# Moving a state space block between the k steps of two projections, with PSUM banks given by hand

## The chip, the cores and the metric

The kernel runs on one core of one Trainium2 chip. The metric is the device time of one execution in microseconds. Before the change the median of three runs is 1287.9 us (1287.57 to 1289.54).

## The reference

A model of two layers on 512 tokens of width 1024. Each layer adds to the stream a mixer, a cross attention to 256 memory rows, and a mixture of experts. The change is in the mixer of the first layer:

```
z = rmsnorm(h) @ w_in                       # 512 x 1024 @ 1024 x 1536
uv = gelu(z[:, :1024])
ya = gmlp(uv[:, :512], uv[:, 512:])         # u * (causal chunk mixing of layernorm(v) + bias)
yb = s5(z[:, 1024:])                        # diagonal complex state space model, 32 groups of 16
h += concat(ya, yb) @ w_out
...
lam_bar = exp(lam * step); bu = uf @ b_bar  # complex states, 64 per group
states = scan(a * state + bu)
y = gelu(real(states @ c) + d * uf)
yb = y * sigmoid(y @ w_glu + b_glu)
```

Everything is fp32. The kernel runs the state space model in chunks of 8 tokens, 64 chunks: inside a chunk a fixed 128 x 128 matrix for each group (s5T) maps inputs to outputs, and only the state at chunk borders is scanned.

## The kernel before

Each engine has its own program, written out by hand, and signals and waits by semaphores. PSUM has eight banks of 128 x 512 fp32. A list, `uses_of_banks`, names every use of a bank in the order of TensorE's program, with a count; without a group the uses go round all eight banks in turn, with a group (a tuple) they take its banks. `claim` lets TensorE wait until the earlier use of the bank was evacuated, `fill` signals the result, `await_filled` waits for it on the reading engine, `evac` gives the bank back, and `taken` waits for that.

Projections of the width 1024 run in `split_gemm`: eight k steps, and in each, for each of the four token tiles, three fp32r passes (high times high, high times low, low times high), so 12 matmuls of 128 x 512 to a step, which accumulate in four banks. The high parts of the weights are made by ScalarE (L1353, `weights`) and the low parts by GpSimd (L659, `low_parts`), into a ring of four steps; a high part waits until the step four earlier was used. `split_gemm` takes `between`, a table from a k step to functions that are called after it; the second layer's mixer uses it already.

The first mixer has three projections: ev2 (the state space input s5u), ev1 (v0) and ev0 (u0). TensorE's order before is: ev2, the transposes into chunks, V (L922, chunk inputs into states, 64 small products), Vsw (L929, the product with `perm`, which exchanges real and imaginary halves, four products of two recorded parts each), the whole of ev1, Xp (L936, the same exchange of the scanned states), y (L945 and L946, chunk outputs: for each of 8 banks four groups, the inputs by s5T and the carried states by s5PP), the whole of ev0, yT (L955), then mixed (L963, the token mixing of the LayerNorm of v).

VectorE multiplies the Vsw banks by sines (L1926), runs the scan and products (L1929 to L1936, `s5_scan`), subtracts the Xp banks (L1942) and signals `s5_x`; then it works on the LayerNorm of v (L1949 to L1959, `vh_ready`), for which ScalarE makes 16 squares (L1482) and a root (L1485). ScalarE copies V (L1409) after `s5_t`, the sixteen-part signal of the eight transfers L605 that build s5T out of memory which V's copy overwrites; it applies Gelu to v0 (L1469), to the eight y banks (L1474), and to u0 (L1490).

In the second layer `mix_norm1` transposes the normalised stream into eight banks (L777), ScalarE and VectorE split each into high (L1345) and low (L1770), and `dq` is the first projection of that mixer, in banks 4 to 7.

Of the kernel before, what the change touches and what calls it, by code (L numbers as in the profile page):

```python
# [27 lines left out]
ACT = mybir.ActivationFunctionType  # L28
# [10 lines left out]
def uses_of_banks(layers):  # L39

    steps = [("cols", 1), ("memT", 4), ("kv0", 2), ("ct", 2), ("kv1", 2), ("kv2", 2), ("bT", 8), ("mix_norm0", 8),
# [3 lines left out]

    def attention(l):
        return [(f"xa_norm{l}", 8), (f"q{l}", 8), (f"qT{l}", 8), (f"sc{l}", 8), (f"pT{l}", 8), (f"o{l}", 8),
                (f"wo{l}", 8)]

    def moe(l):  # L50
        return [(f"ffn_norm{l}", 8), (f"route{l}", 1), (f"logits{l}", 1), (f"rank{l}", 1), (f"idx{l}", 1, (7,)), (f"gslot{l}", 1, (7,))]

    G, O = (1, 2, 3, 4), (5, 6, 7, 0)
    steps += attention(0) + moe(0)
    steps += [("mix_norm1", 8), ("dq", 4, (4, 5, 6, 7)), ("if", 1, (0,)), ("dk", 4, G), ("qk", 4, O), ("col", 1, (1,)),
              ("qk1", 4, G), ("og", 4, O), ("v", 4, G), ("mlh0", 4, O), ("mlh1", 4, O), ("dT", 8, O),
              ("dv", 4, G), ("ms0", 4, O), ("num0", 4, O), ("mlh2", 4, O), ("mlh3", 4, O), ("ms1", 4, O), ("num1", 4, O),
              ("ms2", 4, O), ("mt0", 3, O), ("mt1", 3, O), ("mo0", 1, G), ("ms3", 4, O), ("mo1", 1, G), ("mt2", 3, O),
              ("ycT", 4, O), ("out1", 4, G), ("mo2", 1, O), ("mt3", 3, O), ("mo3", 1, O), ("out1b", 4, O)]
    steps += attention(1) + moe(1)  # L60
    first, bank_of, nth_of = {}, [], []
    used, turn = [0] * 8, {None: 0, G: 0, O: 0}
    for name, k, *group in steps:
        first[name] = len(bank_of)
        for i in range(k):
            g = group[0] if group else None
            if g in turn:
                b = g[turn[g] % 4] if g else turn[g] % 8
                turn[g] += 1
            else:  # L70
                b = g[i]
            bank_of.append(b)
            nth_of.append(used[b])
            used[b] += 1
    return first, bank_of, nth_of


def program(nc, A, out):
# [8 lines left out]
    LC = P // GI  # L87
    NC = T // LC
# [5 lines left out]
    first, bank_of, nth_of = uses_of_banks(2)  # L94
    RING = 4

    ctx = ExitStack()
    with ctx:
# [80 lines left out]
        S = {n: sem(n) for n in names}  # L179
# [8 lines left out]
        def bank(u):  # L188
            return banks[bank_of[u]]
# [15 lines left out]
        def await_filled(eng, u):  # L205
            eng.wait_ge(filled[bank_of[u]], nth_of[u] + 1)

        def evac(ins, u):
            ins.then_inc(evacuated[bank_of[u]], 1)
# [134 lines left out]
        Y = E[2][0:NC, :].rearrange("c (j n) -> c j n", j=LC)  # L344
        s5Wst = v3(hflat, G)
        uT = v3(E[4], 4, 0, 2048)
        yT = v3(E[3], 4, 2048, 4096)
# [111 lines left out]
        xlo = {"ev": v3(E3r, KT), "q": v3(E4r, KT), "o": v3(E1r, KT), "od": v3(E2r, KT), "out1": v3(E5r, KT, 0, KT * T)}  # L459
        xhi, ohi = v3(xTr, KT), v3(E0r, KT)  # L460

        def by_k(buf):
            return [buf[:, k, :] for k in range(KT)]
# [299 lines left out]
        def _(pe):  # L763
# [16 lines left out]
            def split_gemm(u, panel_name, hi, lo, x_ready=None, weights_first=False, between={}):  # L780


                for k in range(KT):
                    s_ = step(panel_name, k)
                    if x_ready:
                        x_ready(k)
                    pe.wait_ge(S["w_lo"], s_ + 1)
                    wh, wl = whi[s_ % RING], wlo[s_ % RING]
                    xh, xl = hi[k], lo[k]
                    for t in range(TT):  # L790
                        if k == 0:
                            claim(pe, u + t)
                        c = slice(t * P, (t + 1) * P)
                        if weights_first:
                            passes = ((wh[:, c], xh), (wh[:, c], xl), (wl[:, c], xh))
                        else:
                            passes = ((xh[:, c], wh[:, :]), (xh[:, c], wl[:, :]), (xl[:, c], wh[:, :]))
                        for n, (a, b) in enumerate(passes):
                            ins = pe.matmul(bank(u + t)[:, :], a, b, start=(k == 0 and n == 0),  # L799
                                            stop=(k == KT - 1 and n == 2))  # L800
                        if k == KT - 1:
                            fill(ins, u + t)
                    if k < KT - 1:
                        ins.then_inc(S["w_used"], 1)
                    for step_between, n in between.get(k, ()):
                        step_between(n)
# [3 lines left out]
            u = first["cols"]  # L810
# [7 lines left out]
            u = first["memT"]  # L818
# [23 lines left out]
            for n, c in enumerate((Cst1, Cst2)):  # L842
                u = first["ct"] + n
# [8 lines left out]
            for n in range(8):  # L852
                u = first["bT"] + n
# [12 lines left out]
            for n in range(8):  # L866
                u = first["w"] + n
# [49 lines left out]
            for n in range(4):  # L917
# [4 lines left out]
                    ins = pe.matmul(bank(u)[:, g * NC:(g + 1) * NC], s5Q[:, 8 * n + g, :], Uc[:, 8 * n + g, :],  # L922
                                    start=(g == 0), stop=(g == 7), skip_group_check=True)
                fill(ins, u)
            for n in range(4):
                u = first["Vsw"] + n
                claim(pe, u)
                taken(pe, first["V"] + n)
                fill(pe.matmul(bank(u)[:, :], perm[:], Vc[:, 8 * n:8 * n + 8, :].rearrange("p g c -> p (g c)"),  # L929
                               start=True, stop=True), u)  # L930
            split_gemm(first["v0"], "ev1", by_k(xhi), by_k(xlo["ev"]))
            pe.wait_ge(S["s5_scan"], 1)
            for n in range(4):
                u = first["Xp"] + n
                claim(pe, u)
                fill(pe.matmul(bank(u)[:, :], perm[:], Vs[:, 8 * n:8 * n + 8, :].rearrange("p g c -> p (g c)"),  # L936
                               start=True, stop=True), u)
            pe.wait_ge(S["s5_x"], 1)
            pe.wait_ge(S["s5_t"], 16 * LC)
            for n in range(8):  # L940
                u = first["y"] + n
                claim(pe, u)
                for g in range(4 * n, 4 * n + 4):
                    o = bank(u)[0:NC, (g % 4) * P:(g % 4 + 1) * P]
                    pe.matmul(o, Uc[:, g, :], s5T[:, g, :], start=(g % 4 == 0), stop=False, skip_group_check=True)  # L945
                    ins = pe.matmul(o, Sc[:, g, :], s5PP[:, g, 1:LC + 1, :].rearrange("p k i -> p (k i)"),  # L946
                                    start=False, stop=(g % 4 == 3), skip_group_check=True)
                fill(ins, u)
            split_gemm(first["u0"], "ev0", by_k(xhi), by_k(xlo["ev"]))
            taken_all(pe, "y", 8)  # L950
            for n in range(4):
                u = first["yT"] + n
# [377 lines left out]
        def _(act):  # L1330
# [16 lines left out]
            def weights(name, k0, k1):  # L1347

                await_panel(act, name)
                for k in range(k0, k1):  # L1350
                    s_ = step(name, k)
                    await_ring(act, s_)
                    act.activation(whi[s_ % RING][:, :], slot(name)[:, k, :], ACT.Copy).then_inc(S["w_hi"], 1)  # L1353
# [112 lines left out]
            for n in range(4):  # L1466
                u = first["v0"] + n
                await_filled(act, u)
                evac(act.activation(Gv[:, n, :], bank(u)[:, :], ACT.Gelu_apprx_tanh), u)  # L1469
            act.wait_ge(S["s5_x"], 1)  # L1470
            for n in range(8):
                u = first["y"] + n
                await_filled(act, u)
                evac(act.activation(Y[:, :, 64 * n:64 * n + 64].rearrange("c j (g i) -> c g j i", g=4),  # L1474
                                    bank(u)[0:NC, :].rearrange("c (g j i) -> c g j i", g=4, j=LC),
                                    ACT.Gelu_apprx_tanh), u)
            for n in range(16):
                if n % 4 == 0:
                    weights("ev0", RING + n // 4, RING + n // 4 + 1)
                if n == 0:  # L1480
                    act.wait_ge(S["ln_mean"], 1)
                a_(act.activation(junk[:, 0:P], Gv[:, n // 4, (n % 4) * P:(n % 4 + 1) * P], ACT.Square,  # L1482
                                  bias=xnm[:, n:n + 1], accum_out=xsum[:, n:n + 1]), "ln_sq")
# [968 lines left out]
```

## Time and profile before

| | us |
|---|---|
| median of three runs | 1287.9 |
| profiled execution, its own time | 1289.58 |
| its span, first to last instruction | 1287.4 |
| TensorE busy (matmul) | 1191.6 |
| VectorE busy | 612.5 |
| ScalarE busy | 500.0 |
| GpSimd busy | 346.8 |
| mean granted TensorE clock | 0.974 of full |

All times below are of the one profiled execution, in microseconds from its first instruction. An entry of the chain of waits gives start, length and what the time was spent in; TensorE's matmuls overlap, so a length in the chain is the time to the next one, while the length in a timeline includes the pipeline's end.

### The profile page before, as it was taken

The numbers are of one execution on the slowest core, as the hardware profiler recorded it, in microseconds if no ns is written. First come the engines' busy times: TensorE is split into PE (matmuls) and PEld (weight loads), VectorE is DVE, ScalarE is ACT, GpSimd is POOL, SyncE is SP. The second block draws the span as 40 slices with busy tenths as digits, with TensorE's granted clock in tenths as the row PEclk, the third lists the DMA queues.
The fourth block names the chain that finished last, engine by engine and source line by source line (L and its number), as shares of the span: only waits on it lengthen the run. The fifth ranks groups of instructions, "written<-read, shape, count | busy, mean of one in ns | idle before, by whom it ended". The sixth has DMA issues, their size and how long they took to land.

```text
span 1287.4 us, 14453 instructions
## 1 busy us (share of the span) xinstructions
PE 1191.6 (93%) x5099; PEld 847.9 (66%) x5099; DVE 612.5 (48%) x1117; ACT 500.0 (39%) x980; POOL 346.8 (27%) x311
## 2 busy tenths in 40 slices
PE   5999899999899799999699999979998997999997
PEld 2467686788667555555477887758887674555554
DVE  5883433320512644445735972772205226444457
ACT  2453146354624323233434354352546343233222
POOL 2023331564022011112134754253350220111120
PEclk9999899999899899999989999999999998999999
DMA  9432221276102899999103221012311017999953
GB/s 267 143 131 74 30 107 66 107 300 247 66 1 96 326 395 369 377 382 339 67 13 126 79 89 42 1 66 69 128 66 66 1 67 314 409 380 379 378 218 142
DMA packets 77639, 222.70 MB, mean 173 GB/s; under 512 B 21708, under 2 KB 22648, under 8 KB 65272
## 3 DMA queue, kind: packets, MB, share of 16 engines
q1 hardware_dynamic: 64688, 180.22, 38.0%
q0 software_dynamic: 10048, 36.74, 7.5%
q10 hardware_dynamic: 2840, 4.91, 1.0%
q8 instruction: 39, 0.64, 0.2%
q14 instruction: 24, 0.20, 0.0%
HBM read 187.90 MB, written 32.51 MB: 171 GB/s over the span
## 4 chain that ended last, share of the span: by engine, by line
PE 77%; DVE 12%; ACT 5%; issue 2%; POOL 1%; SPq 1%; DMA 1%; DVEq 0%; POOLq 0%; ACTq 0%
PE bank L799 37%; PE bank L1114 16%; PE bank L1141 7%; PE bank L1028 2%; PE bank L1069 1%; PE bank L835 1%; DVE h L2202 1%; PE bank L1042 1%; PE bank L972 1%; DVE E2r L2163 1%; PE bank L777 1%; PE bank L1019 1%; PE bank L1164 1%; SPq L605 1%; ACT E2r L1589 1%
## 5 line engine op out<-in xcount | busy, mean ns | idle before, releaser
L659 POOL TENSOR_TENSOR wlo<-W,whi 128x512 fp32r<-128x512 f32 x176 | 255.0, 1461 | 492.2 <-ACT whi L1353 491.8
L1353 ACT ACTIVATE whi<-W 128x512 fp32r<-128x512 f32 x176 | 107.9, 633 | 256.1 <-PE bank L799 249.1
L799 PE MATMUL bank<-whi,xTr 128*128 128x512 f32 x480 | 191.2, 398 | 0.6 <-ACT E L1716 0.6
L799 PE MATMUL bank<-wlo,xTr 128*128 128x512 f32 x416 | 162.7, 391 | 0.0
L1114 PE MATMUL bank<-W,E 128*128 128x512 f32 x256 | 114.4, 601 | 1.9 <-DVE E L2036 1.9
L1114 PE MATMUL bank<-E 128*128 128x512 f32 x256 | 112.4, 592 | 0.0
L799 PEld LDWEIGHTS bank<-whi,xTr 128*128 128x128 f32 x480 | 90.7, 189 | 20.5 <-issue 1.3
L1141 PE MATMUL bank<-whi,E2r 128*128 128x512 f32 x256 | 87.4, 402 | 8.9 <-DVE E2r L2163 8.4
L799 PEld LDWEIGHTS bank<-wlo,xTr 128*128 128x128 f32 x416 | 78.6, 189 | 16.7 <-issue 1.0
L692 POOL COPY idx<-slots 128x1 uint32 (+1 forms) x30 | 5.5, 182 | 307.8 <-PE bank L1103 217.6
L1114 PEld LDWEIGHTS bank<-W,E 128*128 128x128 f32 x256 | 49.0, 193 | 57.9 <-issue 54.4
L1114 PEld LDWEIGHTS bank<-E 128*128 128x128 f32 x256 | 48.7, 190 | 54.7 <-issue 53.5
L1811 DVE TENSOR_TENSOR h<-bank,h 128x512 f32<-128x512 f32 x32 | 21.8, 692 | 131.4 <-PE bank L799 131.4
L1141 PEld LDWEIGHTS bank<-whi,E2r 128*128 128x128 f32 x256 | 48.1, 188 | 25.5 <-issue 10.5
L1589 ACT ACTIVATE E2r<-bank 128x256 fp32r<-128x256 f32 x32 | 12.3, 384 | 132.4 <-PE bank L1124 132.4
L799 PE MATMUL bank<-whi,E0r 128*128 128x512 f32 x160 | 63.1, 395 | 0.0
L799 PE MATMUL bank<-whi,E1r 128*128 128x512 f32 x160 | 62.8, 393 | 0.0
L2163 DVE TENSOR_TENSOR E2r<-bank,E2r 128x256 fp32r<-128x256 f32 x32 | 13.6, 424 | 102.9 <-ACT E2r L1589 102.9
L799 PE MATMUL bank<-whi,E2r 128*128 128x512 f32 x160 | 62.5, 391 | 0.0
L835 PE MATMUL bank<-W,E 128*128 128x512 f32 x128 | 58.8, 621 | 4.0 <-DVE E3r L1770 2.5
L799 PE MATMUL bank<-wlo,E0r 128*128 128x512 f32 x160 | 62.4, 390 | 0.0
L1602 ACT ACTIVATE E<-bank 128x512 f32<-128x512 f32 x26 | 15.5, 597 | 97.1 <-PE bank L1141 97.1
(465 smaller groups left out, 2256.9 us busy)
## 6 DMA issues: line engine op xcount, KB each, us to landing
E<-in_moe_w SPq DMA_DIRECT2D x48, 1024.0 KB, 9.4
W<-in_moe_w SPq DMA_DIRECT2D x32, 1024.0 KB, 9.2
xT<-in_moe_w SPq DMA_DIRECT2D x16, 1024.0 KB, 10.9
W<-in_od_w_in SPq DMA_DIRECT2D x7, 2048.0 KB, 8.4
ybuf<-E SPq DMA_DIRECT2D x26, 512.0 KB, 5.1
ybuf<-memV POOLq DMA_DIRECT2D x12, 1024.0 KB, 19.9
W<-in_w_mem_kv SPq DMA_DIRECT2D x4, 2048.0 KB, 8.1
W<-in_xa_wq SPq DMA_DIRECT2D x4, 2048.0 KB, 7.6
```

Of the source, the lines that this page charges most:

```text
L605: sp.dma_start(s5T[GI * j:GI * (j + 1), :, GI * j:P], s5Wst[0:GI, :, 0:P - GI * j])\
L659: pool.tensor_tensor(wlo[s_ % RING][:, :], slot(name)[:, k, :], whi[s_ % RING][:, :].bitcast(F32), ALU.subtract).then_inc(S["w_lo"], 1)
L799: ins = pe.matmul(bank(u + t)[:, :], a, b, start=(k == 0 and n == 0), stop=(k == KT - 1 and n == 2))
L835: ins = pe.matmul(bank(u)[:, :], memnT[:, k, t * P:(t + 1) * P], slot(f"kv{n}")[:, k, :], start=(k == 0), stop=(k == KT - 1))
L1028: ins = pe.matmul(bank(u)[:, :], memV[:, k, n * XD + d * P:n * XD + (d + 1) * P], pT[:, n, k, :], start=(k == 0), stop=(k == 1))
L1114: ins = pe.matmul(banks[2 + par][:, :], xgT[par][:, k, :], w13s[j][:, :, k, :], start=(k == 0), stop=(k == KT - 1))
L1141: ins = pe.matmul(banks[5 + half][:, :], a, b[:, :], start=(k == 0 and n == 0), stop=(k == 1 and n == 2))
L1353: act.activation(whi[s_ % RING][:, :], slot(name)[:, k, :], ACT.Copy).then_inc(S["w_hi"], 1)
L1589: act.activation(hThi[par], banks[4][:, 0:2 * P], ACT.Copy).then_inc(m["ht_hi"], 1)
L1602: act.activation(yo[par][:, 512:1024], banks[6][:, :], ACT.Copy).then_inc(m["y_ready1"], 1)
L1811: evac(tt(hs, bank(u)[:, :], hs, ALU.add), u)
L2163: tt(hTlo[j % 2], banks[4][:, 0:2 * P], hThi[j % 2].bitcast(F32), ALU.subtract).then_inc(m["ht_ready"], 1)
```

## The change

The exchanges Vsw come after k step 1 of the projection ev1. Xp comes after k step 0 of ev0, and the eight y banks in pairs after its k steps 1 to 4. The banks of V, Vsw, v0, Xp, y and u0 are given by hand. On ScalarE the high parts of ev0's steps 4 and 5 are made ahead of the first y Gelu, each pair of y Gelus stands ahead of a group of four squares, and the high parts of steps 6 and 7 come after the second and third pair.

```
-             ("uc1", 1), ("uj3", 2), ("uc2", 1), ("uc3", 1), ("V", 4), ("Vsw", 4), ("v0", 4), ("Xp", 4), ("y", 8),
-             ("u0", 4), ("yT", 4), ("mixed", 4), ("glu0", 2), ("yaT", 4), ("glu2", 2), ("out0", 8)]
+             ("uc1", 1), ("uj3", 2), ("uc2", 1), ("uc3", 1), ("V", 4, (0, 1, 2, 3)), ("Vsw", 4, (0, 1, 2, 3)), ("v0", 4, (4, 5, 6, 7)),
+             ("Xp", 4, (4, 5, 6, 7)), ("y", 8, (4, 5, 6, 7, 4, 5, 6, 7)), ("u0", 4, (0, 1, 2, 3)), ("yT", 4), ("mixed", 4), ("glu0", 2), ("yaT", 4), ("glu2", 2), ("out0", 8)]
...
-            for n in range(4):
+            def swapped(n):
                 u = first["Vsw"] + n
...
-            split_gemm(first["v0"], "ev1", by_k(xhi), by_k(xlo["ev"]))
-            pe.wait_ge(S["s5_scan"], 1)
-            for n in range(4):
+
+            def swapped_back(n):
...
-            pe.wait_ge(S["s5_x"], 1)
-            pe.wait_ge(S["s5_t"], 16 * LC)
-            for n in range(8):
+
+            def chunk_outputs(n):
+                pe.wait_ge(S["s5_x"], 1)
+                pe.wait_ge(S["s5_t"], 16 * LC)
...
-            split_gemm(first["u0"], "ev0", by_k(xhi), by_k(xlo["ev"]))
+
+            split_gemm(first["v0"], "ev1", by_k(xhi), by_k(xlo["ev"]), between={1: [(swapped, n) for n in range(4)]})
+            split_gemm(first["u0"], "ev0", by_k(xhi), by_k(xlo["ev"]),
+                       between={0: [(swapped_back, n) for n in range(4)], 1: [(chunk_outputs, 0), (chunk_outputs, 1)],
+                                2: [(chunk_outputs, 2), (chunk_outputs, 3)], 3: [(chunk_outputs, 4), (chunk_outputs, 5)],
+                                4: [(chunk_outputs, 6), (chunk_outputs, 7)]})
             taken_all(pe, "y", 8)
...
+            weights("ev0", RING, RING + 2)
             act.wait_ge(S["s5_x"], 1)
-            for n in range(8):
-                u = first["y"] + n
-                await_filled(act, u)
-                evac(act.activation(Y[:, :, 64 * n:64 * n + 64].rearrange("c j (g i) -> c g j i", g=4),
-                                    bank(u)[0:NC, :].rearrange("c (g j i) -> c g j i", g=4, j=LC),
-                                    ACT.Gelu_apprx_tanh), u)
             for n in range(16):
                 if n % 4 == 0:
-                    weights("ev0", RING + n // 4, RING + n // 4 + 1)
+                    for y in (n // 2, n // 2 + 1):
+                        u = first["y"] + y
+                        await_filled(act, u)
+                        evac(act.activation(Y[:, :, 64 * y:64 * y + 64].rearrange("c j (g i) -> c g j i", g=4),
+                                            bank(u)[0:NC, :].rearrange("c (g j i) -> c g j i", g=4, j=LC),
+                                            ACT.Gelu_apprx_tanh), u)
+                if n in (4, 8):
+                    weights("ev0", RING + 1 + n // 4, RING + 2 + n // 4)
```

## Rows read from the trace of the kernel before

**Rows 1.** The page, chain that ended last, shares by engine.

```profile
PE 77%; DVE 12%; ACT 5%; issue 2%; POOL 1%; SPq 1%; DMA 1%; DVEq 0%; POOLq 0%; ACTq 0%
```

**Rows 2.** Busy time by stage: window, length, each engine's busy us (count), clock, DMA.

```profile
core 0: us, PE busy (x) PEld busy (x) DVE busy (x) ACT busy (x) POOL busy (x), PEclk, DMA share, GB/s
129.00:136.50 7.50, 7.21 (x64) 7.07 (x64) 0.00 (x0) 0.56 (x1) 0.00 (x0) 1.00 0.73 95
136.50:140.40 3.90, 0.00 (x0) 0.00 (x0) 0.00 (x0) 0.66 (x2) 0.00 (x0) 0.88 0.39 54
140.40:147.00 6.60, 6.52 (x9) 2.83 (x10) 2.08 (x3) 1.41 (x3) 0.00 (x0) 0.55 0.00 0
149.00:169.00 20.00, 20.00 (x89) 16.49 (x88) 17.56 (x8) 4.56 (x8) 18.26 (x6) 1.00 0.01 1
```

**Rows 3.** Chain that ended last, from V to y: start, length, what.

```profile
136.47 3.25 DMA E<-h
...
140.48 6.57 PE bank L929 x8
147.05 21.79 PE bank L799 x96
168.84 3.45 PE bank L936 x8
...
173.23 0.43 PE bank L945 x2
```

**Rows 4.** Timeline of TensorE, the V products (in brackets idle time and releaser).

```profile
128.85 7.36 PE L922 MATMUL bank<-E 128*128 128x64 f32 x64
```

**Rows 5.** The same chain from u0 on.

```profile
187.42 21.98 PE bank L799 x96
209.40 2.16 PE bank L955 x32
211.56 3.63 PE bank L963 x8
```

**Rows 6.** Timeline of GpSimd, the last low part before V.

```profile
111.85 1.26 POOL L659 TENSOR_TENSOR wlo<-W,whi 128x512 fp32r<-128x512 f32 x1 [1.43 <-ACT whi L1353]
```

**Rows 7.** Timeline of ScalarE, 139 to 202 us.

```profile
139.74 2.06 ACT L1409 ACTIVATE h<-bank 128x512 f32<-128x512 f32 x4 [10.18 <-DMA E<-h]
...
169.52 1.28 ACT L1469 ACT_TABLE_LOAD   x1
170.81 2.07 ACT L1469 ACTIVATE E<-bank 128x512 f32<-128x512 f32 x4
...
187.46 0.59 ACT L1474 ACTIVATE E<-bank 64x512 f32<-64x512 f32 x1 [1.16 <-PE bank L946]
...
191.00 0.39 ACT L1482 ACTIVATE junk<-E,st 128x128 f32<-128x128 f32 x1
...
192.87 0.19 ACT L1482 ACTIVATION_READ_ACCUMULATOR junk<-E,st 128x1 f32 x1
...
201.06 0.18 ACT L1482 ACTIVATION_READ_ACCUMULATOR junk<-E,st 128x1 f32 x1
```

**Rows 8.** Timeline of VectorE: behind the scan, and the last LayerNorm step.

```profile
163.47 3.27 DVE L1936 TENSOR_TENSOR h<-E 128x2048 f32<-128x2048 f32 x1
...
207.73 2.29 DVE L1959 TENSOR_TENSOR E<-E,W 128x2048 f32<-128x2048 f32 x1
```

**Rows 9.** Second mixer: chain pieces between k steps, and two stages with the clock.

```profile
806.35 2.77 PE bank L799 x12
809.12 4.46 PE bank L1265 x40
813.59 2.73 PE bank L799 x12
...
801.00:824.00 23.00, 22.79 (x110) 16.95 (x111) 13.77 (x46) 8.55 (x23) 7.65 (x6) 1.00 0.01 1
824.00:846.00 22.00, 21.33 (x115) 16.80 (x114) 17.88 (x66) 8.96 (x27) 1.26 (x1) 1.00 0.00 1
```

**Rows 10.** mix_norm1 to dq: VectorE's low parts of k=4 to 7, and the chain.

```profile
652.24 2.73 DVE L1770 SCALAR_TENSOR_TENSOR E2r<-bank,cols,xTr 128x512 fp32r<-128x512 f32 x4
...
652.86 21.78 PE bank L799 x96
```

More of the change, by code:

```diff
@@ L930, in _ @@
                                start=True, stop=True), u)
-            split_gemm(first["v0"], "ev1", by_k(xhi), by_k(xlo["ev"]))
-            pe.wait_ge(S["s5_scan"], 1)
-            for n in range(4):
+            def swapped_back(n):
+                pe.wait_ge(S["s5_scan"], 1)
                 u = first["Xp"] + n
```

## The prediction

> **What bounds the kernel now.** I read the page first. The chain that ended last runs through TensorE for 77% of the span and VectorE for 12% [rows 1]: time goes away only where TensorE stands still or runs slowly. So I cut the stretch that the change touches, from the state-input products (L922) to the token mixing (L963), into stages, and looked in each for idle time and clock.
>
> There are three losses in it. After the last V product TensorE idles and then the clock is low: the stage from 136.5 has no matmul at all, and the one from 140.4 ran at a granted clock of 0.55, mostly the lower of its two levels, though the stages before and after are at 1.00 [rows 2]. The chain says what it waited for: the L605 transfers landed at 139.72, ScalarE could then copy V into the space they had been reading, and the eight swap products L929 began at 140.48 and took 6.57 us, where the same eight products with the same operand shapes took 3.45 us later (L936) [rows 3]. V itself ended at 128.85 + 7.36 = 136.21 [rows 4]. The third is the wait behind L936: it ended at 172.29 and L945 began at 173.23 [rows 3]. From there to L963 TensorE has no gap: y, u0 and the transposes stand end to end [rows 3, 5].
>
> The times from 136.21 to 211.56, where L963 starts, are: 4.27 idle, 6.57 swap, 21.79 v0, 3.45 swap back, 0.94 idle, 14.19 y (173.23 to 187.42), 21.98 u0, 2.16 yT; together 75.35, as it must be [rows 3, 5].
>
> **The change part by part.** *Swaps between k steps 1 and 2 of v0.* Steps 0 and 1 of ev1 wait for nothing late: their banks 4 to 7 were last used by uc0, uj2 and uc1, which had to be evacuated for V to be computed, and the ring's first four low parts were made by 113.1, before V [rows 6]. One k step is 12 matmuls, 21.79/8 = 2.72 us [rows 3], so two fill 136.21 to 141.66. ScalarE copies V from 139.74 to 141.80 [rows 7], one bank each 0.52 us, so the first swap (141.66) finds bank 0 done and each next one too. The 4.27 us idle goes. TensorE never stands still, so I take the swap at the full-clock 3.45 us: 3.12 less. V moves from banks 4 to 7 to 0 to 3, free since uj3, uc2, uc3: nothing. Behind the waiting swap only v0's steps 2 to 7 are queued; the ring feeds them: ScalarE starts on step 4 at 141.8, and it is needed at 145.11 + 5.45 = 150.6.
> v0 ends at 136.21 + 3.45 + 21.79 = 161.45.
>
> *Swap back behind step 0 of u0.* Its vector chain starts when the swaps are evacuated, at about 146.2 instead of 147.9, and so s5_scan, which came with L1936's start at 163.47 [rows 8], comes near 161.8. u0's step 0 ends at 164.17, so the wait is covered. New is that the swap back uses v0's banks and must wait for the Gelu of v0: before, v0 ended at 168.84 and the first Gelu began, behind a high part and a table load of 1.28 us, at 170.81, 0.52 each [rows 3, 7]. So bank 4 is free 2.5 us after v0's end, at 163.95, 0.2 us before it is wanted, and the others follow faster than the 0.86 us of a product. Cost 0. Without step 0 as cover this would be 2.5 us; if the claim waited for all four Gelus it would be 161.45 + 4.04 - 164.17 = 1.3 us, the upper bound.
>
> *y in pairs behind steps 1 to 4.* The 0.94 us wait goes: the swap back ends at 167.62, VectorE finishes it 0.7 us later, and y starts only after step 1, at 170.35. y has four banks instead of eight; a bank is wanted again a whole k step after its pair, while its Gelu is finished 0.6 us after its fill (187.42 to 188.05 for the last) [rows 7]. Nothing again. The high parts of steps 4 to 7 now stand between the y Gelus in ScalarE's queue, as do four squares after each pair; the latest, step 7, is made after y5's Gelu (about 187.5), and TensorE wants it near 199. Covered by 10 us.
>
> *Returns to the projection.* Each piece between ends with a change of operand kind. After the swap v0 took 21.79 us, eight plain steps; after y u0 took 21.98, so that return cost 0.19 [rows 3, 5]. In the second mixer, built this way already, the step after 40 L1265 products took 2.73, that after L1275 2.77 or less: 0.01 to 0.05 [rows 9]. I take 0.19 for the four returns after y, the same pair of instructions, of which one existed: 0.57 added, with 0.05 for three more (0.15) and 0.19 for five more (0.95) as the bounds. The Trainium skill (TensorE: Matmul & The Clock Gate, "Step-by-step: what each phase is for") says that weight loads are pulled ahead of running matmuls; by that a return would be free and the sum 0.57 us better. The 21.98 here says otherwise after y.
>
> u0 ends at 161.45 + 21.79 + 3.45 + 14.19 + 4 x 0.19 = 201.64 instead of 209.40; yT ends at 203.80.
>
> *What is late next: the LayerNorm.* It used to be hidden under u0. vh_ready needs all 16 squares, and the last four now stand behind the Gelus of y6 and y7. y7 is filled three steps and a return before u0's end: 201.64 - 8.17 - 0.19 = 193.28. Gelu 0.64, four squares 2.06 (191.00 to 193.06) [rows 7]. From the last square to vh come the root, the reciprocal, 16 scalings and the gain: the squares ended at 201.24 and L1959 at 207.73 + 2.29 = 210.02, so 8.8 us [rows 7, 8]. So 193.28 + 0.64 + 2.06 + 8.8 = 204.8, against 203.80: L963 waits 1.0 us. Bounds: 0, and 1.7, a third of the 2.06 us of squares more. L963 starts at 204.8 instead of 211.56: **6.8 us earlier**. Behind it the order is as before.
>
> *The banks elsewhere.* The six uses given by hand took 28 turns, so each later use in plain rotation moves by four banks. In the first layer every use moves alike and meets its old predecessor. Where the rotation meets groups fixed by hand it doesn't: mix_norm1 had k 0 to 7 in banks 3,4,5,6,7,0,1,2 and now has 7,0,1,2,3,4,5,6, and dq stands in 4 to 7. dq's first tile needed the evacuation of k=1, and will need that of k=5, its second k=6, its third k=7. VectorE did k=4 to 7 from 652.24 to 654.97, so k=5 is done at about 653.65, k=6 at 654.3; dq began at 652.86 [rows 10]. So **0.85 us later**; the tiles follow at 0.68 each and find 654.3 and 654.97 met. Bounds 0.8 and 2.1 (all evacuated first). xa_norm1 also moves against out1b, but its transposes come after the evacuations either way: 0.
>
> The SP queue only gets its signals sooner (glu panel with v0's end, x again with s5_x), and the panels are wanted later than they land: 0.
>
> **Sum.** -4.27 - 3.12 - 0.94 + 0.57 + 1.0 + 0.85 = -5.9 us. The profiled execution's span 1287.4 becomes 1281.5 and its own time 1289.58 becomes 1283.7. The median of the runs is 1287.9, 1.7 under that execution, and my time is **1282.0**.
>
> **Rivals.** *A, new waits eat half.* The margin of 0.2 us before the swap back is thin, and dq may wait for all evacuations: +1.3, +1.25, +0.7 in the LayerNorm, 3.25 if all comes, so up to 1285.3. Against it: the Gelu and evacuation rows are steady. *B, v0's first steps don't start early,* because a bank, a panel or a low part is late: then the idle time and the low clock stay and the costs come all the same: -0.94 + 0.57 + 1.0 + 0.85 = +1.5, so 1289.4. Nothing in the profile speaks for it. *C, slower: the clock falls in the interleaved stretch.* Place: from u0's step 0 to step 4. Work at the lower of the two levels (1.2 instead of 2.4 GHz) takes twice the time, as the swaps show (6.57 against 3.45). If only the 14.19 us of y ran so, the time would be 1282.0 + 14.2 = 1296.2; from 8.5 us of such work on the kernel is slower beyond what can be told. For it: a TensorE that moves between banks, with a wait at each piece. Against it: the second mixer does the same with six kinds of pieces, and its stretches from 801 to 846 were at 1.00 in spite of a wait [rows 9]. The Trainium skill (TensorE: Matmul & The Clock Gate, "A second HAM failure mode: psum-queue depth-cycling") speaks against the change: it tells of a kernel that cycled through PSUM banks and whose small idles made the clock swing. By that rule it would be C; the stretches of [rows 9] weigh more.
>
> **How the numbers follow.** The forecast has 0.74, A 0.14, B 0.05, C 0.04, and 0.03 is for more gain than forecast. The forecast's own range is 1280.8 to 1283.5 (returns and LayerNorm at their bounds, and half a us for where clock changes fall elsewhere). The three runs spread by 2 us; a difference under 0.2%, 2.6 us, can't be told from none. A reaches to 1285, and the range is 1280.4 to 1285.0. Faster by over 0.2% is all of the forecast and most of A, 0.90; the same 0.06; slower 0.04.
>
> **What would show it.** Right: TensorE busy without a gap from 128.9 to about 204, L929 near 3.5 us at clock 1.00, v0 ending near 161.5, u0 near 201.6, a wait of about 1 us for L1959 at L963, one of about 0.8 us before dq, and everything else moved rigidly. Wrong: a wait at L936 for the Gelu of v0 or at y for L1942, a clock under 1 between 141 and 204, u0's steps well over 2.72 us, or a later stage that gives the time back.

## The result, and the profile after

Five runs of the changed kernel had a median of 1281.13 us (1280.2 to 1283.53), five of the kernel before 1288.69; the ratio is 0.9943, with a 95% interval from 0.9931 to 0.9956. Two later comparisons of the same two kernels gave 0.9949 (0.9935 to 0.9962) and 0.9948 (0.9934 to 0.9962). By the three ratios the change takes off 6.6 to 7.4 us; 5.9 were forecast. The profiled execution took 1280.32 us with a span of 1278.1, 9.3 less than the span before, and this pair of traces is taken apart below, since 9.3 is more than the runs bear out.

The chain that ended last in the changed kernel, from V on (start, length, what; L922 V, L929 and L936 the two exchanges, L946 and L947 y, L961 yT, L969 the token mixing):

```profile
127.33 7.29 PE bank L922 x64
134.62 5.55 PE bank L799 x24
140.17 3.43 PE bank L929 x8
143.60 19.05 PE bank L799 x84
...
162.66 3.67 PE bank L936 x8
166.33 2.75 PE bank L799 x12
169.09 0.36 PE bank L946 x2
...
172.72 2.94 PE bank L799 x12
...
192.46 8.38 PE bank L799 x36
200.85 2.16 PE bank L961 x32
203.01 0.94 issue
203.95 3.67 PE bank L969 x8
```

The idle time of [rows 3] is gone, and the first exchange takes 3.43 us instead of 6.57. TensorE stands still only once, 0.94 us ahead of L969. From V's end to L969 it is 203.95 - 134.62 = 69.33 us instead of 75.35, 6.02 less. The busy time by stage (window, length, busy us by engine with counts, clock, DMA) shows full clock all the way, where [rows 2] had 0.55:

```profile
127.40:134.60 7.20, 7.20 (x65) 7.20 (x66) 0.00 (x0) 0.57 (x1) 0.00 (x0) 1.00 0.73 95
...
140.10:143.60 3.50, 3.50 (x10) 1.58 (x9) 2.08 (x3) 1.20 (x3) 2.50 (x2) 1.00 0.01 2
...
162.60:192.40 29.80, 29.79 (x186) 24.10 (x185) 5.95 (x8) 13.36 (x38) 8.15 (x6) 1.00 0.29 106
```

What the wait of 0.94 us is for stands in the timelines of ScalarE and VectorE: the last y Gelu, and the last step of the LayerNorm (L1967 here, L1959 in [rows 8]), which ends at 203.85, 0.1 us before L969 starts:

```profile
192.50 0.59 ACT L1483 ACTIVATE E<-bank 64x512 f32<-64x512 f32 x1 [1.09 <-PE bank L947]
...
201.56 2.29 DVE L1967 TENSOR_TENSOR E<-E,W 128x2048 f32<-128x2048 f32 x1
```

Ahead of dq the chain now goes over VectorE:

```profile
633.33 5.16 DVE E L1792 x4
...
638.53 3.05 PE bank L777 x13
...
642.32 2.10 DVE E2r L1778 x3
...
644.56 1.61 PE bank L799 x6
```

From the start of the scaling (L1792, before L1784) to dq it is 11.23 us. In the trace of before the chain goes from the scaling over the transposes straight to dq at 652.86 [rows 10], and 652.86 - 642.39 = 10.47, so dq comes 0.76 us later than it did:

```profile
642.39 5.16 DVE E L1784 x4
647.59 5.27 PE bank L777 x29
```

The whole difference of the two profiled spans, cut at V's end, L969, the scaling and dq, is then -1.6 (136.21 to 134.62) - 6.0 - 1.5 + 0.8 - 1.0 = -9.3 us. In that order the pieces are: up to V's end, V to L969, L969 to the scaling, the scaling to dq, and behind dq. The touched pieces make -5.3; the other -4.0 (1.59 + 1.45 + 1.00) lie in stages whose instructions did not change.

### The profile page after: what moved, and what is told of

Its sections match the earlier page's. It is cut to its first block, busy times and chain, and to the rows that moved or that the text cites. A ratio compares the mean times of both kernels' runs of the same rounds, so it can differ in the third digit from the quotient of the medians.

```text
span 1278.1 us, 14465 instructions
## 1 busy us (share of the span) xinstructions
PE 1185.6 (93%) x5099; PEld 843.2 (66%) x5099; DVE 612.1 (48%) x1117; ACT 500.6 (39%) x980; POOL 347.5 (27%) x311
## 4 chain that ended last, share of the span: by engine, by line
PE 78%; DVE 12%; ACT 5%; issue 3%; POOL 1%; DMA 1%; DVEq 0%; POOLq 0%; ACTq 0%
PE bank L799 37%; PE bank L1120 16%; PE bank L1147 7%; PE bank L1034 2%; PE bank L1075 2%; PE bank L1048 1%; PE bank L835 1%; DVE h L2210 1%; PE bank L978 1%; DVE E2r L2171 1%; PE bank L1170 1%; ACT E2r L1597 1%; PE bank L1025 1%; PE bank L1281 1%; PE bank L777 1%
## 5 line engine op out<-in xcount | busy, mean ns | idle before, releaser
L1120 PE MATMUL bank<-W,E 128*128 128x512 f32 x256 | 112.9, 594 | 1.9 <-DVE E L2044 1.9
L835 PE MATMUL bank<-W,E 128*128 128x512 f32 x128 | 57.4, 609 | 3.7 <-DVE E3r L1778 2.2
```

The costliest lines, as they stand in the source:

```text
L835: ins = pe.matmul(bank(u)[:, :], memnT[:, k, t * P:(t + 1) * P], slot(f"kv{n}")[:, k, :], start=(k == 0), stop=(k == KT - 1))
L1120: ins = pe.matmul(banks[2 + par][:, :], xgT[par][:, k, :], w13s[j][:, :, k, :], start=(k == 0), stop=(k == KT - 1))
```

## The experiments

All ratios are to runs of the kernel before on the same chip. Where a figure says V to mixing, it is the time from the end of V (L922) to the start of the token mixing, 75.35 us before and 69.33 changed.

**The first exchange alone.** The exchange moves behind k step 1 of v0; the swap back, y and u0 keep their old order.

```
-             ("uc1", 1), ("uj3", 2), ("uc2", 1), ("uc3", 1), ("V", 4), ("Vsw", 4), ("v0", 4), ("Xp", 4), ("y", 8),
-             ("u0", 4), ("yT", 4), ("mixed", 4), ("glu0", 2), ("yaT", 4), ("glu2", 2), ("out0", 8)]
+             ("uc1", 1), ("uj3", 2), ("uc2", 1), ("uc3", 1), ("V", 4, (0, 1, 2, 3)), ("Vsw", 4, (0, 1, 2, 3)), ("v0", 4, (4, 5, 6, 7)),
+             ("Xp", 4, (0, 1, 2, 3)), ("y", 8, (4, 5, 6, 7, 0, 1, 2, 3)), ("u0", 4, (4, 5, 6, 7)), ("yT", 4, (0, 1, 2, 3)), ("mixed", 4), ("glu0", 2), ("yaT", 4), ("glu2", 2), ("out0", 8)]
...
-            split_gemm(first["v0"], "ev1", by_k(xhi), by_k(xlo["ev"]))
+            split_gemm(first["v0"], "ev1", by_k(xhi), by_k(xlo["ev"]), between={1: [(swapped, n) for n in range(4)]})
```

> Only the first exchange (L929 of before) moves between k steps 1 and 2 of v0; swap back, y and u0 keep their old order, and banks are given so that every later use has its old bank. Theory: the 4.3 us idle and the 3.1 us of low clock go, so v0 ends 7.4 us earlier, but the scan on VectorE comes only 1.7 us earlier, so the swap back and y wait for it for about 2.4 us: 5.0 us less than before, no change before dq. Rival 1: the whole gain of the change is in this move, 7.4 us less. Rival 2: the gain is due to the second half of the change, no gain here.

Measured: ratio 0.9955 (0.9942 to 0.9969), median 1282.59. Chain:

```profile
136.10 5.54 PE bank L799 x24
141.65 3.45 PE bank L929 x8
...
161.52 3.25 DVE h L1937
...
164.98 2.46 DVE E L1943 x4
...
167.67 0.43 PE bank L946 x2
...
183.53 22.01 PE bank L799 x96
...
207.70 3.63 PE bank L964 x8
```

Busy time by stage, the first part of y:

```profile
167.60:172.30 4.70, 4.63 (x28) 4.63 (x29) 2.46 (x2) 0.59 (x1) 0.00 (x0) 0.65 0.79 257
```

The exchange is as cheap as forecast, and now the chain runs over VectorE's scan. The wait ahead of y, 2.7 us, was foreseen; not foreseen was that it brings the clock down, so that y took 183.53 - 167.67 = 15.86 us instead of 14.19. V to mixing is 71.60, 3.75 less than before instead of the 5.0 expected. Rival 1 falls in the trace: this half needs the other one to hide the scan. The times alone would not exclude rival 1: the interval reaches from 4.0 to 7.5 us. The measured 5.8 us lies above the trace's 3.75; the traced execution is the slowest of its five (1284.90), so the others need not have had the drop at y. The second half of the change is worth 71.60 - 69.33 = 2.3 us by the traces, and 1.4 when its 0.9 ahead of dq is taken off; the times of this version and of the changed kernel overlap and don't show it.

**The u0 part alone.** The first exchange is called four times in front of v0, as before; all else is the changed kernel.

```
-            split_gemm(first["v0"], "ev1", by_k(xhi), by_k(xlo["ev"]), between={1: [(swapped, n) for n in range(4)]})
+            for n in range(4):
+                swapped(n)
+            split_gemm(first["v0"], "ev1", by_k(xhi), by_k(xlo["ev"]))
```

> The first exchange goes back in front of v0; swap back and y pairs stay between the steps of u0, banks as in the changed kernel. Theory: the idle time and low clock are back, and what this half saves (0.94 us in front of y) is less than it costs (entries and returns around each piece, about 1.0 to 1.5, LayerNorm wait 0.9, dq 0.8): 1.5 to 2.5 us slower than before. Rival 1: this half is worth 2 us or more by itself, faster than before. Rival 2: neither, within 0.5 us.

Measured: ratio 1.0009 (1.0000 to 1.0018), median 1289.42. Chain:

```profile
140.60 6.28 PE bank L929 x8
146.88 24.52 PE bank L799 x108
...
211.78 0.93 issue
212.71 3.67 PE bank L971 x8
```

From the first exchange's start to the mixing it is 72.11 us, before 211.56 - 140.48 = 71.08: 1.0 more, and the banks ahead of dq come on top, 11.32 us from the scaling to dq instead of 10.47. That is 1.9 us in the trace, as expected. The time rose by about 1.2 us (0 to 2.3), at the edge of what can be told. So this half alone gains nothing; in the changed kernel its use is to stand over the scan.

**The idle time filled.** The order of before, with five more products in the gap:

```
+            claim(pe, first["Vsw"])
+            for _ in range(5):
+                pe.matmul(bank(first["Vsw"])[:, :], perm[:], s5Q[:, 0:4, :].rearrange("p g c -> p (g c)"),
+                          start=True, stop=True)
```

> The kernel before with five more products of the exchange's shape (128 x 512 fp32) in the idle time between V and the first exchange, into the bank that the exchange overwrites; order and banks unchanged. They add work and change no result. Theory: the idle time ends no earlier, but the clock stays up and the exchange takes 3.45 instead of 6.57 us: 3.1 us less than before. Rival 1: the exchange is slow for another reason (its operand just copied, the waits in between), then it stays at 6.57 us and the time is the same or up to 0.3 us longer. Rival 2: the five products run into the exchange's start and eat the gain.

Measured: ratio 0.9977 (0.9968 to 0.9986), median 1285.08. Chain (L927 the added products, L933 the exchange):

```profile
134.53 4.35 PE bank L927 x10
138.88 3.65 PE bank L933 x8
...
207.06 3.63 PE bank L967 x8
```

Busy time by stage, the exchange:

```profile
138.90:142.50 3.60, 3.60 (x9) 1.69 (x10) 2.08 (x3) 1.27 (x3) 0.00 (x0) 1.00 0.00 0
```

With more work the kernel is faster by 3.0 us. The exchange itself is 2.9 us shorter, at a clock of 1.00 instead of 0.55, and V to mixing is 72.53 us, 2.8 less. The exchange starts 4.35 us behind V's end instead of 4.27, so the added products delay it by only 0.1 us, and both rivals fall. That the first exchange was slow by the clock, and the clock low by the idle time, is shown. The Trainium skill (TensorE: Matmul & The Clock Gate, "HAM oscillation — how this bites in real kernels") says that idle gaps throttle the engine again; here the traces agree, with a clock of 0.55 behind the idle 4.27 us and 1.00 where they are filled.

**The banks alone**, in the order of before.

```
-             ("uc1", 1), ("uj3", 2), ("uc2", 1), ("uc3", 1), ("V", 4), ("Vsw", 4), ("v0", 4), ("Xp", 4), ("y", 8),
-             ("u0", 4), ("yT", 4), ("mixed", 4), ("glu0", 2), ("yaT", 4), ("glu2", 2), ("out0", 8)]
+             ("uc1", 1), ("uj3", 2), ("uc2", 1), ("uc3", 1), ("V", 4, (0, 1, 2, 3)), ("Vsw", 4, (0, 1, 2, 3)), ("v0", 4, (4, 5, 6, 7)),
+             ("Xp", 4, (4, 5, 6, 7)), ("y", 8, (4, 5, 6, 7, 4, 5, 6, 7)), ("u0", 4, (0, 1, 2, 3)), ("yT", 4), ("mixed", 4), ("glu0", 2), ("yaT", 4), ("glu2", 2), ("out0", 8)]
```

> The order of before with the changed kernel's bank list. Theory: the swap back must wait for the Gelus of v0 without a k step as cover, 2.5 us, and dq begins 0.8 us late: 3.3 us slower than before. Rival 1: the banks cost nothing, same time. Rival 2: y on four banks waits for its own Gelus as well, 5 us or more slower.

Measured: ratio 1.0033 (1.0021 to 1.0045), 4.2 us slower. Chain:

```profile
170.33 0.61 ACT E L1469
...
171.07 3.69 PE bank L936 x8
```

The swap back waits for v0's first Gelu, until 171.07, 2.7 us behind v0's end at 168.36. Step 0 of u0 as cover is what makes these banks free in the changed kernel, where L936 follows at once. y takes 14.19 us again (175.70 to 189.89), so rival 2 falls. V to mixing is 2.5 us more than before, and the scaling to dq 0.9 more: the trace has 3.4 of the 4.2 us.

**The changed kernel again, and the kernel before again.**

> The changed kernel once more, as the base for the three kernels run with it. Theory: 7 us less than before, of which 5.3 are made in the stages that the change touches and the rest by where the clock falls in stages that it does not touch; so this execution's trace should show 5.3 us again in the touched stages and another figure elsewhere. Rival: the other 2 us are a lasting effect of the moved banks, and come again in the same stages.

> The changed kernel a third time. Theory: 5 to 6 us less than before, 76.7 us from V's first product to L963, the drop near 70 us there or not. Rival: again 6.5 us or more, so that something outside the touched stages gains steadily.

> The kernel before once more as a candidate of its own. Theory: ratio 1.000 to the other runs of before within 0.15%; its trace shows the same low clock at 140 us, and the drops near 70 and 450 us may be there or not, 1.6 us each. Rival: these drops are in every execution of before, then they belong to this kernel and the changed one has rid itself of them.

Measured: the changed kernel 0.9949 and 0.9948, the kernel before 0.9998 (0.9989 to 1.0007). V to mixing is 69.32 and 69.30 us in the two new traces of the changed kernel, so in the changed kernel this stretch repeats to 0.1 us. In the second trace of before it is 74.94 instead of 75.35, because the exchange took 6.12 us instead of 6.57. Dq came 11.20 and 11.41 us behind the scaling in the new traces of the changed kernel, and 10.35 in that of before. Over all pairs the touched stages make 4.6 to 5.3 us. What does not repeat is shown by one window of the first trace of before, whose code no kernel here changes,

```profile
60.00:80.00 20.00, 17.53 (x85) 11.35 (x84) 19.54 (x29) 15.14 (x37) 4.97 (x4) 0.91 0.29 105
```

and the same window of the changed kernel:

```profile
60.00:80.00 20.00, 17.83 (x90) 11.71 (x89) 19.54 (x29) 15.16 (x37) 4.98 (x4) 1.00 0.29 105
```

V starts at 128.7 to 128.9 where the first kind is met and at 127.2 or 127.3 where the second is. Of 14 traces 8 have the one and 6 the other: both of before, and one of three of the changed kernel, have the drop. It is worth the 1.6 us of the first piece above. The -1.5 us between L969 and the scaling are the sum of three. In the first trace of before they are these rows of the chain (32 transposes of the attention, 64 small products, 16 products of an expert):

```profile
345.49 6.43 PE bank L1019 x32
...
430.06 8.81 PE bank L1069 x64
...
450.34 8.70 PE bank L1114 x16
```

In the first trace of the changed kernel the same instructions took 5.35, 9.96 and 7.13 us: -1.1, +1.2 and -1.6. The last is a drop of the clock at 440 to 460 us (0.91 against 1.00); four of the 14 traces have it, and in just these the 64 products ahead of it took 8.7 to 9.0 us instead of 9.9 to 10.3, so most of what it costs is given back. The transposes took 6.43 and 6.20 us in the traces of before and 5.35 in all three of the changed kernel, but 6.62 in the version with the lowest median below. Behind dq the changed kernel took 633.5, 636.1 and 633.7 us, before 634.5 and 634.4; the long one is in the execution of 1284.68 us, whose unchanged stages together gained nothing.

The theory of these experiments is confirmed for the touched stages. For the whole kernel the rival's number holds, again 6.6 us or more; that its cause is the moved banks is not shown, and the banks alone speak against it, since their time rose by more than their trace has. Three comparisons gave 6.6 to 7.4 us, and 4.6 to 5.3 are accounted for. The mean granted clock, which is on record for most executions, bears on the rest. The share of the full clock that was not granted, times the span, is on average 30.9 us in 51 executions of before and 26.2 us in the 15 of the changed kernel (mean clock 0.976 and 0.980). By [rows 2] the stages around the first exchange make 3.4 of these 4.7 us. So 1.3 us, an estimate with an error of 0.5, were gained by the clock in other stages. But the version with the idle time filled, with 25.9 us, shows the same gain and is not faster than its trace explains, so this does not show the cause of the rest either.

**y in one block.**

```
-                       between={0: [(swapped_back, n) for n in range(4)], 1: [(chunk_outputs, 0), (chunk_outputs, 1)],
-                                2: [(chunk_outputs, 2), (chunk_outputs, 3)], 3: [(chunk_outputs, 4), (chunk_outputs, 5)],
-                                4: [(chunk_outputs, 6), (chunk_outputs, 7)]})
+                       between={0: [(swapped_back, n) for n in range(4)], 1: [(chunk_outputs, n) for n in range(8)]})
...
-                if n % 4 == 0:
-                    for y in (n // 2, n // 2 + 1):
+                if n == 0:
+                    for y in range(8):
```

> The changed kernel with all eight y banks behind k step 1 of u0 and all eight Gelus ahead of the squares. Theory: three entries and three returns less, 1.0 us, and the LayerNorm is ready before u0 ends, so its wait of 0.9 us goes: 1.9 us less than the changed kernel. Rival 1: y on four banks in one block waits for its Gelus: up to 2 us more. Rival 2: the wait for the LayerNorm comes from something else and stays: 1.0 us less.

**mix_norm1's banks as before.**

```
-    steps += [("mix_norm1", 8), ("dq", 4, (4, 5, 6, 7)), ("if", 1, (0,)), ("dk", 4, G), ("qk", 4, O), ("col", 1, (1,)),
+    steps += [("mix_norm1", 8, (3, 4, 5, 6, 7, 0, 1, 2)), ("dq", 4, (4, 5, 6, 7)), ("if", 1, (0,)), ("dk", 4, G), ("qk", 4, O), ("col", 1, (1,)),
```

> The changed kernel with the banks of mix_norm1 given by hand as they were before the change. Theory: dq starts right behind the transposes again, 0.8 us less than the changed kernel. Rival: dq waits for something else too, no difference in the trace.

**Both.**

> Both edits, y in one block and mix_norm1's banks as before. Theory: the two add up, 2.7 us less than the changed kernel, 8.0 us less than before in the touched stages. Rival: they cover each other or the time is made up again later, 1 us less or nothing.

Measured beside the changed kernel's 1282.45 (0.9949): 1281.04 (0.9944, 0.9930 to 0.9958) for one block, 1282.73 (0.9949, 0.9936 to 0.9963) for the norm banks, 1280.99 (0.9942, 0.9929 to 0.9956) for both edits. The intervals overlap, so the times tell none of them from the changed kernel; the traces do. Chain of the one-block version:

```profile
136.28 5.53 PE bank L799 x24
...
170.73 0.36 PE bank L946 x2
...
184.85 16.54 PE bank L799 x72
...
203.55 0.67 issue
204.22 5.37 PE bank L967 x8
```

V to mixing is 67.94 us, 1.4 less than the changed kernel, of the 1.9 expected. y took 184.85 - 170.73 = 14.12 us, so its banks cost no wait and rival 1 falls. The entries and returns are saved, but the wait for the LayerNorm only fell from 0.94 to 0.67 us. With all squares behind the last Gelu it is 16 of them, not four, that stand between y and the root; that I had left out. Chain of the version with mix_norm1's banks alone, ahead of dq:

```profile
635.95 5.16 DVE E L1792 x4
...
641.15 5.13 PE bank L777 x29
646.29 3.90 PE bank L799 x17
```

The VectorE piece is gone from the chain, and the scaling to dq takes 10.34 us instead of 11.23: the banks cost 0.9 us there, as forecast. With both edits V to mixing is 67.96 us and the scaling to dq 10.43, so in the trace the savings add up to 2.2 us, of the 2.7 expected; the medians differ by 1.5, which the intervals don't tell from nothing.

**Squares between the Gelus.** Both edits, and on ScalarE two squares behind each y Gelu:

```
             for n in range(16):
+                if n % 2 == 0:
+                    u = first["y"] + n // 2
+                    await_filled(act, u)
+                    evac(act.activation(Y[:, :, 32 * n:32 * n + 64].rearrange("c j (g i) -> c g j i", g=4),
...
             a_.n["ln_sq"] += 1
+            weights("ev0", RING + 2, RING + 4)
```

> Y in one block and mix_norm1's banks as before, and now two of the LayerNorm's squares behind each y Gelu, the root right behind them, and the high parts of steps 6 and 7 after the root. Theory: in the version with both edits the LayerNorm still came 0.67 us late because 16 squares stood behind the last Gelu; now its root runs 8 us earlier, the wait in front of L963 goes and the stage from V to L963 is 0.7 us shorter than in that version, 74.6 us from V's first product instead of 75.3; some 9 us less than before in the touched stages. Rival 1: the wait has another cause and stays at 0.67 us. Rival 2: the high parts of steps 6 and 7 come late and TensorE waits inside u0.

Measured: ratio 0.9946 (0.9932 to 0.9960), median 1280.46, the lowest of all. Chain:

```profile
134.53 5.55 PE bank L799 x24
...
183.09 16.54 PE bank L799 x72
...
201.80 3.63 PE bank L967 x8
```

The wait is gone, so it was the LayerNorm's. V to mixing is 67.27 us, 2.1 less than the changed kernel, and u0's steps run without a gap. That it is faster as a whole the runs don't show: 1280.46 beside 1280.87 for the changed kernel in the same comparison, and beside 1280.99 for both edits without this one. Its trace has the drop at 440 us and the long transposes in the attention.

**One step of cover less.**

```
-            split_gemm(first["v0"], "ev1", by_k(xhi), by_k(xlo["ev"]), between={1: [(swapped, n) for n in range(4)]})
+            split_gemm(first["v0"], "ev1", by_k(xhi), by_k(xlo["ev"]), between={0: [(swapped, n) for n in range(4)]})
```

> The changed kernel with the first exchange behind k step 0 of v0 instead of step 1, so one step of cover less. Theory: ScalarE's copy of V sets the start, TensorE idles about 1.5 us, the clock stays up, and everything behind is 1.5 us later than in the changed kernel. Rival 1: the short idle time is enough to bring the clock down, then 3 us more on top. Rival 2: one step of cover is enough, no difference.

Measured: median 1285.16, ratio 0.9985 (0.9972 to 0.9998). Chain:

```profile
138.88 3.67 PE bank L929 x8
```

Busy time by stage, around the idle time:

```profile
137.00:139.00 2.00, 0.50 (x3) 0.16 (x2) 0.00 (x0) 0.87 (x2) 0.00 (x0) 1.00 0.16 21
```

TensorE idled 1.5 us in that window and the clock stayed at 1.00; the exchange took 3.67. From V's end to L936 it is 1.8 us more than in the changed kernel, which fits the theory that the copy of V sets the start, and the second step of cover is worth that. The traced execution, 1284.34, is 3.5 us slower than that of the changed kernel in the same comparison, and the trace has them: 1.8, and 1.7 in the mixing, which took 5.37 instead of 3.67 us at a clock of 0.68 behind the same 0.94 us wait. The medians differ by 4.3 us; the runs reached up to 1292.37, and the rest is open.

## Why the prediction was right

*The idle time and the clock, -4.27 and -3.12.* Right, and each shown by itself. With the gap filled the exchange is 2.9 us shorter, of the 3.1, though it starts no earlier. Two steps and the first exchange took 5.55 + 3.43 = 8.98 us, forecast 8.90.

*The swap back at no cost behind step 0.* Right: no wait at L936, though the margin was 0.2 us; the banks alone cost 2.7 us there without the cover.

*y, and the returns.* The 0.94 us went. The returns were nearly as priced (2.94 for a step behind a y pair, 2.72 + 0.2). Missing were the entries, the first products of each piece. The pair that opens a piece of y takes 0.36 instead of 0.22 us; the one block of before had one such pair too, of 0.43, so the eight y banks grew by 4 x 3.63 - 14.19 = 0.3 us. The exchange inside u0 took 3.67 instead of 3.45, another 0.2, the six k steps behind y 0.14 more than the sum has, and the first exchange with its two steps 0.1. That is 0.8 us that the sum did not have, and why V to mixing fell by 6.0 and not 6.8.

*The LayerNorm wait, +1.0.* Right: 0.94, and it is the LayerNorm, since it goes to 0 when the squares are moved.

*dq, +0.85.* Right: 0.76 between the two traces, 0.89 against the version with the old banks, up to 1.06 over all traces of the two kernels.

*Rival C*, the clock falling in the interleaved stretch, did not come: 1.00 from 162.6 to 192.4 in spite of four banks taken in turn. The Trainium skill's rule on cycling through PSUM banks (TensorE: Matmul & The Clock Gate, "A second HAM failure mode: psum-queue depth-cycling") tells of a TensorE that often stands still for a moment between groups of products. Here it did not (29.79 of 29.80 us busy), so the stretch shows that four banks in turn do not by themselves bring the clock down, and not what such idles would do. Rivals A and B did not come either.

*The total.* Forecast -5.9, touched stages -4.6 to -5.3, measured -6.6 to -7.4. The mechanism was right in every step in the touched stages. The term with the wrong size is the one that I put at half a us, where the clock changes fall elsewhere: in the profiled pair it is 4.0 us, so the sign "everything else moved rigidly" did not come. That the median of 1281.1 lies within 1 us of the 1282.0 forecast is in part luck, since the touched stages gave less than forecast and the others more. Part of it is chance, as the traces of the same kernel show. Some 1.3 to 2.8 us come back in each of three comparisons; whether the shift itself makes the low clock rarer in other stages stays open, and the 14 traces can't settle it. The lower end of the forecast's own range doesn't follow from its bounds: returns, LayerNorm and clock give 1282.0 - 0.42 - 1.0 - 0.5 = 1280.1, not 1280.8.

## What to carry to other kernels

A wait of a few us on TensorE can cost twice, once as idle time and again as work at low clock; put a piece of the neighbouring projection over it, and count which result gets late next, because the piece that depends on the moved one may then be the wait: here the move of the u0 part gained nothing alone and was still what covered the scan. Count the entries and returns of each piece (0.36 us here for a piece of y), and keep pieces whole where the reader can keep up. When banks are given by hand, follow the rotation to the next group that is fixed by hand: that cost 0.9 us, at a place more than 400 us further on.

## What the runs showed of the hardware that was not expected

Idle time does not always bring the clock down, and the same length not always the same: 1.5 us ahead of an exchange left it at 1.00, 2.4 us ahead of y (both idle times as the timeline has them) brought 0.65, and the wait of 0.7 to 0.9 us ahead of the mixing, in eight traces, left the mixing at 3.67 us in six and made it 5.37 in two. Where a drop falls is not fixed by the program: with the same instructions the stretch from 60 to 80 us ran at 0.91 in some executions and at 1.00 in others, 1.5 us apart.
